# Linear attention's levels: where the exponents lie and in which order VectorE and ScalarE take them

## The reference, cut to what matters

```python
b = jnp.cumsum(gi, axis=2)                        # log decays, summed within a chunk of 64
diff = b[:, :, :, None, :] - b[:, :, None, :, :]
decay = jnp.exp(jnp.where(causal, diff, -jnp.inf))
attn = jnp.einsum('bhid,bhjd,bhijd->bhij', qi, ki, decay)
o = einsum(attn, vi) + einsum(qi * jnp.exp(b), S)
S_new = jnp.exp(b_last)[..., None] * S + einsum(ki * jnp.exp(b_last - b), vi)
```

## Time and profile before

| | |
|---|---|
| median of 3 runs | 2382.76 us (2382.25 to 2383.23) |
| profiled execution | 2380.65 us, span 2378.8 us |
| busy | PE 2231.9, PEld 1805.4, DVE 1169.7, ACT 883.9, POOL 856.3 us |
| mean granted TensorE clock | 0.978 of full |

### The profile page before, as it was taken

The page is one execution under the profiler, slowest core; times in us unless marked ns, Lnnn a source line. Parts: engine busy times, 40 slices in busy tenths (PEclk is TensorE's granted clock), DMA queues, the critical chain, the costliest instruction groups (busy, mean ns, idle before and its releaser), DMA issues.

```text
span 2378.8 us, 25562 instructions
## 1 busy us (share of the span) xinstructions
PE 2231.9 (94%) x10350; PEld 1805.4 (76%) x10350; DVE 1169.7 (49%) x1671; ACT 883.9 (37%) x1350; POOL 856.3 (36%) x378
## 2 busy tenths in 40 slices
PE   3999899978999997999999999999999899999997
PEld 2777678866888886766688888887777788888886
DVE  3575442537766304444446654146665532666501
ACT  3221542234343224343444343254444433434322
POOL 2422334442444442421144444443222234444442
PEclk9997999988999998999999999999999999999999
DMA  3211222321333332211133333332111122333332
GB/s 132 80 54 36 66 64 87 108 74 63 98 98 98 96 94 76 77 39 46 44 95 95 97 96 98 96 107 63 57 43 52 54 72 96 98 98 98 93 98 84
DMA packets 56308, 191.43 MB, mean 80 GB/s; under 512 B 6256, under 2 KB 6400, under 8 KB 56064
## 3 DMA queue, kind: packets, MB, share of 16 engines
q1 hardware_dynamic: 56192, 189.81, 25.5%
HBM read 187.69 MB, written 2.10 MB: 80 GB/s over the span
## 4 chain that ended last, share of the span: by engine, by line
PE 86%; DVE 7%; ACT 3%; DMA 2%; issue 1%; SPq 0%; POOL 0%; ACTq 0%; DVEq 0%
PE ps L540 24%; PE ps L542 24%; PE ps L541 24%; PE ps L887 3%; PE ps L957 2%; DMA RAW<-weights 2%; PE ps L864 2%; PE ps L878 1%; PE ps L587 1%; PE ps L588 1%; PE ps L589 1%; ACT WHI L1031 1%; DVE QRHL L1948 1%; DVE KT L1406 1%; PE ps L671 1%
## 5 line engine op out<-in xcount | busy, mean ns | idle before, releaser
L532 POOL TENSOR_TENSOR WLO<-RAW,WHI 128x1024 fp32r<-128x1024 f32 (+2 forms) x374 | 856.1, 2296 | 1495.0 <-ACT WHI L1031 1494.2
L1031 ACT ACTIVATE WHI<-RAW 128x1024 fp32r<-128x1024 f32 (+2 forms) x374 | 372.0, 1000 | 683.4 <-DMA RAW<-weights 514.0
L540 PE MATMUL ps<-HH,WHI 128*128 128x512 f32 x1200 | 479.5, 400 | 15.3 <-DVE HL L1409 9.1
L541 PE MATMUL ps<-HL,WHI 128*128 128x512 f32 x1200 | 470.2, 392 | 0.0
L542 PE MATMUL ps<-HH,WLO 128*128 128x512 f32 x1200 | 469.9, 392 | 0.0
L540 PEld LDWEIGHTS ps<-HH,WHI 128*128 128x128 f32 x1200 | 227.4, 189 | 70.9 <-issue 22.8
L1409 DVE SCALAR_TENSOR_TENSOR CV<-U,PAR,CV 128x512 f32<-128x512 f32 x264 | 265.2, 1025 | 7.0 <-ACT CV L1233 2.3
L541 PEld LDWEIGHTS ps<-HL,WHI 128*128 128x128 f32 x1200 | 227.5, 190 | 49.5 <-issue 3.4
L542 PEld LDWEIGHTS ps<-HH,WLO 128*128 128x128 f32 x1200 | 227.1, 189 | 48.1
L1406 DVE TENSOR_TENSOR U<-ps,RSTD 128x512 f32<-128x512 f32 x132 | 90.5, 688 | 247.4 <-PE ps L542 224.7
L540 PE MATMUL ps<-ACTH,WHI 128*128 128x512 f32 x528 | 205.4, 389 | 0.0
(11 more groups left out here) (288 smaller groups left out, 3370.1 us busy)
## 6 DMA issues: line engine op xcount, KB each, us to landing
RAW<-weights SPq DMA_DIRECT2D x300, 512.0 KB, 3.5
RAW<-weights SPq DMA_DIRECT2D x48, 384.0 KB, 3.0
RAW<-weights SPq DMA_DIRECT2D x26, 256.0 KB, 2.6
X<-xT SPq DMA_DIRECT2D x1, 2048.0 KB, 10.3
outT<-X SPq DMA_DIRECT2D x8, 256.0 KB, 2.1
RESET<-resets SPq DMA_DIRECT2D x1, 512.0 KB, 11.8
CS<-rope SPq DMA_DIRECT2D x1, 512.0 KB, 3.5
M8F<-masks SPq DMA_DIRECT2D x1, 448.0 KB, 9.0
```

The lines of the kernel that those rows point to most:

```text
L532: pool.tensor_tensor(WLO[:, slot, 0:cols], RAW[:, slot, 0:cols], WHI[:, slot, 0:cols].bitcast(F32), ALU.subtract).then_inc(w_lo, 1)
L540: pe.matmul(out, wh, hh, start=first, stop=False)
L541: pe.matmul(out, wh, hl, start=False, stop=False)
L1031: act.activation(WHI[:, slot, 0:cols], RAW[:, slot, 0:cols], ACT.Copy).then_inc(w_hi, 1)
```

## The change

EX becomes a view of PSUM banks 6 and 7 (its place in SBUF stays empty). VectorE's `next_level` is taken apart: `begin_level` holds the wait and the subtractions, and stands one level ahead of `operands`. On ScalarE each exponential stands ahead of weight casts that it was behind: level 2 ahead of the casts of pu2 and pu3, level 3 ahead of sv, and so on. The subtraction after level 6 moves ahead of the drain of sq0 and `select(6)`.

```diff
-        EX = tmp("EX", [P, 2 * T])
+        tmp.at += 2 * T * 4
...
+        EX = ps[:, 6:8, :].rearrange("p a t -> p (a t)")
...
             casts(chunk_of("pu0"))
             gla_level(1)
+            casts(chunk_of("pu1"))
+            gla_level(2)
             casts(chunk_of("pu3"))
-            gla_level(2)
+            gla_level(3)
             casts(chunk_of("sv"))
-            gla_level(3)
+            gla_level(4)
             casts(chunk_of("sq0"))
-            gla_level(4)
+            gla_level(5)
             casts(chunk_of("sq1"))
-            gla_level(5)
+            gla_level(6)
             casts(chunk_of("sq2"))
-            gla_level(6)
...
-            def next_level(level):
+            def begin_level(level):
                 if level > 1:
                     dve.wait_ge(g_lev, level - 1)
                 exponents(LEVELS[level - 1]).then_inc(g_ex, 1)
-                operands(level)
...
-            next_level(1)
+            begin_level(1)
             select(0)
+            operands(1)
+            begin_level(2)
             drain("pu0", FT[:, F_PU, :])
             select(1)
-            next_level(2)
+            operands(2)
+            begin_level(3)
             drain("pu1", FT[:, F_PU + 1, :])
             select(2)
-            next_level(3)
+            operands(3)
+            begin_level(4)
...
             select(5)
-            next_level(6)
+            operands(6)
+
+            dve.wait_ge(g_lev, 6)
+            b = BC[:, :].rearrange("p (c s) -> p c s", s=GLA_CHUNK)
+            dve.tensor_tensor(EX.rearrange("p (c s) -> p c s", s=GLA_CHUNK),
+                              b[:, :, GLA_CHUNK - 1:GLA_CHUNK].broadcast_to([P, 2 * NCHUNK, GLA_CHUNK]), b, ALU.subtract
+                              ).then_inc(g_ex, 1)
             drain("sq0", FT[:, F_SQ, :], 0.125)
             select(6)
-
-            dve.wait_ge(g_lev, 6)
...
             dve.wait_ge(g_dec, 7)
             dve.wait_ge(g_s, 2 * 7)
```

More of the change, by code:

```diff
@@ L1078, in gla_level @@
                 act.wait_ge(g_ex, level)
-                act.activation(EX[:, :], EX[:, :], ACT.Exp).then_inc(g_dec, 1)
+                act.activation(EX, EX, ACT.Exp).then_inc(g_dec, 1)
             casts(chunk_of("q1"))
@@ L1108, in _ @@
             act.wait_ge(g_kd, 1)
-            act.activation(EX[:, :], BC[:, :], ACT.Exp).then_inc(g_dec, 1)
+            act.activation(EX, BC[:, :], ACT.Exp).then_inc(g_dec, 1)
             casts(chunk_of("r1"))
@@ L1474, in exponents @@
                 b = BC[:, :].rearrange("p (n h s) -> p n h s", h=2, s=size)
-                x = EX[:, :].rearrange("p (n h s) -> p n h s", h=2, s=size)
+                x = EX.rearrange("p (n h s) -> p n h s", h=2, s=size)
                 nb = T // size
@@ L1493, in operands @@
                     dve.wait_ge(g_s, 2 * level)
-                mul(QT[:, :], EX[:, :], FT[:, F_Q:F_Q + 2, :].rearrange("p a t -> p (a t)"))
-                mul(KT[:, :], EX[:, :], FT[:, F_K:F_K + 2, :].rearrange("p a t -> p (a t)")).then_inc(g_lev, 1)
-            def next_level(level):
+                mul(QT[:, :], EX, FT[:, F_Q:F_Q + 2, :].rearrange("p a t -> p (a t)"))
+                mul(KT[:, :], EX, FT[:, F_K:F_K + 2, :].rearrange("p a t -> p (a t)")).then_inc(g_lev, 1)
+            def begin_level(level):
                 if level > 1:
@@ L1525, in _ @@
             dve.wait_ge(g_dve, 3)
-            next_level(1)
+            begin_level(1)
             select(0)
+            operands(1)
+            begin_level(2)
             drain("pu0", FT[:, F_PU, :])
             select(1)
-            next_level(2)
+            operands(2)
+            begin_level(3)
             drain("pu1", FT[:, F_PU + 1, :])
             select(2)
-            next_level(3)
+            operands(3)
+            begin_level(4)
             drain("pu2", FT[:, F_PU + 2, :])
             select(3)
-            next_level(4)
+            operands(4)
+            begin_level(5)
             drain("pu3", FT[:, F_PU + 3, :])
             select(4)
-            next_level(5)
+            operands(5)
+            begin_level(6)
             drain_by_token("sv", SV[:, :, :], (0, NT), P, RCOL)
             select(5)
-            next_level(6)
+            operands(6)
[4 more added lines that the diff above has]
+                              ).then_inc(g_ex, 1)
             drain("sq0", FT[:, F_SQ, :], 0.125)
             select(6)
-            dve.wait_ge(g_lev, 6)
[L1547 to L1550, removed]
             dve.wait_ge(g_dec, 7)
             dve.wait_ge(g_s, 2 * 7)
-            mul(KT[:, :], EX[:, :], FT[:, F_K:F_K + 2, :].rearrange("p a t -> p (a t)")).then_inc(g_kd, 1)
+            mul(KT[:, :], EX, FT[:, F_K:F_K + 2, :].rearrange("p a t -> p (a t)")).then_inc(g_kd, 1)
             drain("sq1", FT[:, F_SQ + 1, :], 0.125)
             dve.wait_ge(g_dec, 8)
-            mul(QT[:, :], EX[:, :], FT[:, F_Q:F_Q + 2, :].rearrange("p a t -> p (a t)")).then_inc(g_qe, 1)
+            mul(QT[:, :], EX, FT[:, F_Q:F_Q + 2, :].rearrange("p a t -> p (a t)")).then_inc(g_qe, 1)
             dve.wait_ge(g_kt, 1)
```

## The result

| | before | after |
|---|---|---|
| median | 2383.69 us (6 runs, 2382.25 to 2391.69) | 2371.43 us (6 runs, 2367.68 to 2373.73) |
| profiled execution | 2380.65 us, span 2378.8 us | 2373.73 us, span 2371.9 us |

The ratio of the changed kernel to the one before is 0.9939, with a 95% interval of 0.9921 to 0.9957: 12.3 us less between the medians, whose quotient is 0.9949. In 8 of its 42 runs on record the kernel before took 2391 to 2397 us, at a mean granted clock of 0.972 to 0.974 where it is known, and none of the 18 runs of the changed kernel left 2366 to 2375 us; the cause is open. The forecast was 2371.3 us, and 11.5 us less.

A forecast was written before the change was run, and what follows sets the result against it. TensorE, busy 2231.9 of 2378.8 us, was taken as the bound. Its 62.28 us from level 0 to 6 less 50.75 without waits gave 11.5 off 2380.65: 2369.1, or 2371.3 against the median; range 2367.5 to 2375.5.

The forecast's parts named there:

- The chain from S to the operands: VectorE, from S, the start of a level's scores on TensorE, to the next operands: 6.04 us of 7.6, 1.5 to spare.
- The products don't wait for GpSimd with EX in PSUM: In VectorE's chain at each level, the KT product, 3374 ns in the median before, should take 1.22 us.
- Rival 1: VectorE's products are still held back by GpSimd with EX in PSUM: 4 us of gain lost, time 2375; chance 0.09.
- TensorE's period: TensorE from one level's scores to the next: 1.99 us of scores plus 5.59 of a group, 7.6 us.
- The sum: TensorE, scores of level 0 to level 6: 62.28 us before, 50.75 without waits; difference 11.5, about 1.7 of it low clock.
- The unknown costs: VectorE's and ScalarE's writes to PSUM in the levels, taken at SBUF durations; twice as long would lose 1.7 us.
- rival 3: VectorE's work on EX is stretched by the two PSUM banks: even at factor 2.1, 2400 us at 3; chance 0.04.
- The clock in the outputs' stage: TensorE's outputs, clock 0.56 from 209 to 233 us before: where it falls is unknown, 1.5 us allowed each way.
- GpSimd against the subtractions: GpSimd's remainders meet VectorE's subtractions once, at level 3: 0.6 us of delay, inside the 2.9 to spare.
- Nothing is late next: Behind the levels all engines keep their distance from TensorE, so the 11.5 us shift should stay to the end.
- the step on the rest: Stages behind the levels keep the 11.5 us; wrong if the gain at level 6 is larger than at the end.
- rival 2: Stages behind give back 3 to 7 of 11.5 us, through low clock or heads' waits; about 2376 us; chance 0.08.

The follow-up runs named there:

- e5: Changed kernel with one more VectorE product ahead of each level's two; median 2372.56 us, ratio 0.9942 to the kernel before.
- e6: Changed kernel with two more VectorE products ahead of each level's two; median 2374.50 us, ratio 0.9950 to the kernel before.
- e3: Changed kernel with EX back in SBUF, both new orders kept; median 2375.83 us, ratio 0.9951 to the kernel before.
- e8: Changed kernel again, unedited, one run; 2368.98 us.
- e4: Changed kernel with ScalarE's order of before, exponentials behind the weight casts; median 2372.25 us, ratio 0.9942 to the kernel before.
- e9: Changed kernel with TensorE's outputs dealt out by head between the r groups; median 2360.02 us, ratio 0.9900 to the kernel before.
- e7: Changed kernel with GT, used in the heads' norms, in PSUM bank 7 instead of SBUF; median 2367.77 us, ratio 0.9921 to the kernel before.

## Why the prediction was right

**The chain from S to the operands.** Worked out 6.04 us; measured 106.28 to 111.14 + 1.20 = 112.34, 6.06. Its slack, 1.5 us, is confirmed by e5 and e6.

**The products don't wait for GpSimd with EX in PSUM.** Confirmed by the seven KT products of 1200 to 1234 ns; at level 2 the QT and the KT product both run while GpSimd does. e3 is the counter-test, where they are up to 3.38 us again. Rival 1 fell.

**TensorE's period.** Taken as 1.99 + 5.59 = 7.58, it is 7.65 to 7.69. The sum was 50.75 us for the stage, measured 51.17: the gain in the stage is 11.1 us, not 11.5. A block of scores starts 0.32 us behind the start of a group's last matmul (113.61 to 113.93), where the matmuls of a group follow each other by 0.23, so some 0.09 us per group were left out. The sum also has some 1.7 us for the low clock in the levels. That the clock would be up without the waits was my estimate: it is 1.00 from 98 to 170 us in the changed kernel, and 1.00 over the same stretch in e3 with a wait of 2.5 us and in e6 with five of up to 1.2 us. What brought it down before, no run shows.

**The unknown costs.** VectorE's subtraction into PSUM takes 0.69 to 0.70 us, in SBUF 0.67 to 0.68; ScalarE's exponential from PSUM to PSUM 1.01, in SBUF 1.06. A product from PSUM takes 1.20 to 1.23, from SBUF 1.22 or 1.23. So rival 3, which needed twice the time, was far off. The exponential is thus 0.05 us quicker, where some 0.1 was guessed, and the two products are not longer from PSUM than from SBUF. The clock in the outputs' stage, the other unknown, stayed inside its 1.5 us: 0.59 to 0.61 over 24 us in the four profiles, 0.56 before. How long it lasts differed between executions of the same code: 0.50 from 202 to 225 us in the first profile, from 203 to 222 in e8.

**GpSimd against the subtractions.** Forecast at level 3 alone with 0.6 us; it was level 3 alone with 0.3 us. The casts that stand ahead elsewhere keep clear of it, and e4 shows what it costs where they don't.

**"Nothing is late next", the shift stays to the end.** Right in the medians (12.3, 12.7 and 13.4 us in three comparisons, a little over the 11.5) and wrong as a statement on one execution. By the prediction's own signs the step on the rest fails in the first profile: the gain is 11.3 us at level 6 and 6.9 at the end, and the stage behind takes over 2 us longer. That is rival 2, which had 0.08, in one execution. I held the stages behind to be tied to TensorE alone. But VectorE instructions that read SBUF there are held beside GpSimd's (YGL 2.75 us in place of 0.69), and which comes first hangs on when a transfer lands. In the first profile 4.3 us are lost, 2.6 with such an instruction and the low clock behind it (0.85) and 1.6 with the low clock later (0.89). The forecast of the profiled execution, 2369.1 us, was 4.6 us too low for that reason. That the number for the median came out within 0.2 us is partly luck: the stage gave 0.4 us less than worked out, the medians differ by 0.8 more, and the median of the kernel before is 2383.69 over six runs, not 2382.76.

## What to carry to other kernels

Look at the least and the median duration of the same instruction: the factor of nearly three here (KT, 1221 and 3374 ns) was a wait inside an instruction, which the table of waits did not show as such. VectorE instructions with one input in PSUM ran beside GpSimd at full speed here (KT 1.20 us), those with two inputs in SBUF did not (KT 3.37 us, YGL 2.75 for 0.69), nor did YGH, with one input in SBUF (1.4 us for 0.43). So free PSUM banks were a place for temporaries. Work out each engine's length per period and stop when the chain is under the bound: two remedies worth 7.9 and 7.5 us gave 11.1. A third on the same chain would give nothing, by the same sum; no run tries one.

## What was not expected of the hardware

TensorE's clock can be low in a stretch in which it never stands still: in the block of outputs it is busy for 24.00 of 24.00 us at a granted clock of 0.59, and with the same matmuls in four pieces between groups of 128x512 it is 1.00 (e9). That was worth 9.9 us between the medians, almost as much as the change. What in the block brings it down, the width of the matmuls or something else, no run shows.

And the engines do not meet in semaphores alone, as the description of the chip above has it. A VectorE instruction that reads SBUF can be held by one of GpSimd's, and no line of the program fixes their order: the same YGL took 0.69 us in one execution and 2.75 in another, by when a chunk of weights had landed. With GT in PSUM (e7) it took 0.69 us at 254.14 too, beside a remainder from 254.20 to 256.60.
